# Leaving masked block pairs out of the value products of a hybrid decoder layer, with the last stage in another order

## What is computed

```python
def masked_softmax(s, mask):
    s = jnp.where(mask, s, -jnp.inf)
    ...
    e = jnp.exp(s - m)
    d = jnp.sum(e, axis=-1, keepdims=True)
    return e / jnp.where(d > 0, d, 1.0)
...
# branch "s": selected blocks of 64; SEQ is 1024, so all 16 of them are selected
ms = (top_v > -jnp.inf)[..., None] & (tok <= q_pos[None, :, None, None, None])
...
o_s = jnp.einsum('bqkgns,bqknsd->bqkgd', ps.astype(q.dtype), g[..., 1, :])
# branch "w": sliding window of 512
mw = ((dist >= 0) & (dist <= WINDOW) & (kw_pos[None, :] >= 0))[None, :, None, None, :]
...
o_w = jnp.einsum('bqkgl,blkd->bqkgd', pw.astype(q.dtype), kv_w[:, :, 1])
```

## Time and profile before

| | us |
|---|---|
| median of 3 runs | 885.97 |
| lowest and highest | 880.46, 892.27 |
| span of the profiled execution | 878.0 |
| PE, DVE, ACT, POOL busy in it | 822.5, 520.0, 359.6, 259.9 |

### The profile page before, as it was taken

How to read it: one execution, slowest core, us unless ns; L and a number is a source line. 1 busy time by engine, 2 the same in 40 slices (tenths; PEclk the granted TensorE clock), 3 DMA queues, 4 the chain that set the end, 5 groups by cost and what they waited for, 6 DMA issues and landing times. The chain is left out here.

```text
span 878.0 us, 20078 instructions
## 1 busy us (share of the span) xinstructions
PE 822.5 (94%) x8505; PEld 539.5 (61%) x8505; DVE 520.0 (59%) x1095; ACT 359.6 (41%) x739; POOL 259.9 (30%) x216
## 2 busy tenths in 40 slices
PE   3999999999999999998999998888999989889996
PEld 2457998877788756657555556544646464654553
DVE  2146652376788744457435456686877867757711
ACT  4041002011222245547223337775765656444632
POOL 2048879360000043326311010446211130302021
PEclk8899999999999999999999999899999999999999
DMA  9952265454020000301942452801011010202021
GB/s 302 343 195 104 66 212 206 197 190 165 28 74 1 25 5 1 97 1 49 367 166 62 146 173 63 256 19 29 24 49 51 13 63 6 72 2 74 15 99 49
DMA packets 45411, 89.06 MB, mean 101 GB/s; under 512 B 4388, under 2 KB 26076, under 8 KB 43210
## 3 DMA queue, kind: packets, MB, share of 16 engines
q1 hardware_dynamic: 38202, 54.94, 19.3%
q0 software_dynamic: 6080, 31.79, 10.3%
q10 hardware_dynamic: 1040, 1.05, 0.4%
HBM read 75.49 MB, written 16.40 MB: 105 GB/s over the span
## 5 line engine op out<-in xcount | busy, mean ns | idle before, releaser
L2198 PE MATMUL PS<-W,hT 128*128 128x512 f32 x256 | 113.0, 594 | 0.5 <-DVE W L1819 0.5
L1984 DVE CUSTOM_DVE_ANT_0 PS<-PS,consts 128x640 f32<-128x640 f32 (+5 forms) x96 | 77.3, 837 | 28.7 <-PE PS L2617 28.4
L1103 POOL TENSOR_TENSOR Q<-Q,U 128x512 f32<-128x512 f32 x16 | 20.3, 1268 | 228.4 <-DVE U L2018 228.4
L2198 PEld LDWEIGHTS PS<-W,hT 128*128 128x128 f32 x256 | 47.9, 190 | 56.1 <-issue 54.8
L1431 ACT ACTIVATE hT<-PS,small 128x128 f32<-128x128 f32 (+7 forms) x64 | 47.1, 744 | 47.0 <-DVE small L1984 44.0
L2584 PE MATMUL PS<-U,Y 128*128 128x512 f32 x128 | 60.2, 604 | 0.8 <-ACT Y L1445 0.8
L2584 PE MATMUL PS<-U,Q 128*128 128x512 f32 x128 | 59.3, 601 | 1.3 <-issue 1.3
L1431 ACT ACTIVATE T<-PS,small 128x640 f32<-128x640 f32 (+4 forms) x64 | 41.9, 667 | 30.1 <-DVE small L1984 29.2
L2000 DVE STREAM_TRANSPOSE hT<-hT 128x1024 f32<-128x1024 f32 (+6 forms) x29 | 42.5, 1483 | 2.7 <-ACT hT L1431 2.6
L2584 PEld LDWEIGHTS PS<-U,Q 128*128 128x128 f32 x128 | 23.4, 190 | 32.1 <-issue 32.1
L2617 PE MATMUL PS<-KTsw,W 64*128 64x512 f32 (+3 forms) x128 | 39.4, 519 | 1.6 <-ACT hT L1431 1.3
(11 more groups left out here) (545 smaller groups left out, 1855.3 us busy)
## 6 DMA issues: line engine op xcount, KB each, us to landing
W<-in_w_in SPq DMA_DIRECT2D x4, 2048.0 KB, 7.7
W<-in_w_ada SPq DMA_DIRECT2D x7, 1024.0 KB, 16.1
U<-in_x_prompt SPq DMA_DIRECT2D x8, 512.0 KB, 11.3
W<-in_w_ada SPq DMA_DIRECT2D x2, 2048.0 KB
U<-in_state_win_kv POOLq DMA_DIRECT2D x8, 512.0 KB
W<-in_x_prompt SPq DMA_DIRECT2D x8, 512.0 KB, 3.5
out_y_prompt<-W SPq DMA_DIRECT2D x8, 512.0 KB, 3.4
out_new_win_sample<-in_state_win_kv POOLq DMA_DIRECT2D x1, 4032.0 KB, 24.1
```

Source lines behind the costliest of these rows:

```text
L1103: nc.gpsimd.tensor_tensor(Q3[:, i, :], Q3[:, i, :], spare, ALU.add).then_inc(s_added, 1)
L1984: ins = nc.vector.tensor_tensor_reduce(x, x, strip(u), 1.0, -NEG, ALU.add, ALU.min, sneg_m[u % 2][:, m:m + 1])
L2198: ins = nc.tensor.matmul(bank(z_bank(u)), hT3[:, k, i * P:(i + 1) * P], w, start=(k == 0), stop=(k == KT8 - 1))
```

## The change

A step of a value group leaves out the pairs (j, b) that the mask empties. A new function says which key blocks query block j needs, and the first and last of them carry start and stop:

```diff
+        def key_blocks(u, again, j):
+
+            if again == VALUE_TILES[u] - 1:
+                return 0, j + 1
+            if u % 2 and u // 2 >= WIN // P and again == 0:
+                return j, 4
+            return 0, 4
...
                     for b in range(4):
                         for j in range(4):
+                            lo, hi = key_blocks(u, again, j)
+                            if not lo <= b < hi:
+                                continue
                             q, c = slice(32 * j, 32 * j + 32), again * P + 32 * b
                             for kv in range(KVH):
                                 ins = nc.tensor.matmul(bank(4 + j, 0, P)[HALF[kv]].rearrange("p (g q) -> p g q", g=GQ),
                                                        VREP[k, a + again][q, b * P + kv * HD:b * P + kv * HD + HD],
                                                        PROB[k][q, kv * GQ:kv * GQ + GQ, c:c + 32],
-                                                       start=(again == 0 and b == 0), stop=(last and b == 3))
+                                                       start=(again == 0 and b == lo), stop=(last and b == hi - 1))
```

And ORDER is another string with the same letters, each as often as before:

```diff
-            "qqssxsxyxwmtsvcxtqksysxvxcszsxxwkgstmstxvvcsaxykuwsxtmootooogaxtoootssrrvxppvctxtskusvxtpvxsvcqxopos"
-            "xsostppxpxqpkttsnsyorxoogxottosrvvvttcxsknxavsvvvcstxtuwsxxoqsstmkoxxftosstxoxossgoxtxooyrsrvxvssfvt"
-            "vxcaxstxwmkussxxvvststvvxxvsscxqkxosxtosnsoyxosxtstooxwxssrtgoxxossmrxvvxvsastvvtcxxkussvvxxtnsxvssf"
-            "xvsxxsxvyvsstcoxxqwossmotoxosxgstttoxroxaokssrnxvvxvsstvvctxxkussfxvvtvsxvsxvxvvssctooxtsxgtxsoxorks"
-            "sxvvvxsxvvcatytssoxouoxoftrssoxkoooxsnsrwtxoxossgomxxorbasxvvstsxvvxstxduttvvofvnhvcokvvfovvvcorkogo"
-            "obaodurnhofoooroooornhf")
+            "sqqxsswxysxmvstxtcxyzsqkxtcxtsvsgxmkxcwtsavvysswxuxgkttsopaopoxomrorooxtoscptvvtskusxvvvxpcpspsqxxpo"
+            "potxskxqttxtoyssrtonoosxxstcroxgosvvtvtkxsavscvxvvtsufxxwskxmotnsoxssyoxtgttxoqxstrsorooxosxanstxvvs"
+            "svvxsctsxwfxmukssxxtxvvxscgxstvtxftxyvvsxorxxsotstsoxxmqkossorxoxwsasocxoxstsvvssvvtvkusxsxvntxvsxtx"
+            "sxxcyvxxtxsxvmssvgvssqkoossaofxtwsstxtrooooorxsvtxvnscxsvtvvxskussxxvvxxgssvxxcvfxssvtvvaxtstsotkour"
+            "xxooxcssvyxvmvsnsvvxswrsooxkotooxosxtgsxoossxorooottrbsasxvvsxxsbvvsxtduvvoxvvtnocfvvcvtodthkvvookgf"
+            "aoooounrohroooroofnorhf")
```

## The result

| | before | after |
|---|---|---|
| median of 20 runs each, us | 886.18 (878.41 to 892.27) | 875.81 (871.95 to 881.55) |
| ratio, 95% interval | | 0.9889 [0.9869, 0.9910] |
| span of the profiled execution, us | 878.0 | 879.7 |

The change makes the kernel 9.8 us faster by the ratio, 10.4 by the medians: 1.1%, less than the 2% that the chances were put to, yet its interval is clear of 1. Forecast were -7.8 us and 878.2.

What follows compares the result with a forecast made beforehand. PE was taken to bound the last stage, its dense value steps limited by instruction packets. Terms -8 - 1 + 2 - 0.8 = -7.8 us gave span 870.2 and median 878.2 us (chance 0.48), range 868 to 890.

Steps and rivals of the forecast that it cites:

- the 2% that the chances were put to: Whole kernel: change distinguishable from none, 17.7 us; faster by more 0.10, slower 0.04, within 0.86.
- Term 1: Value products in the last stage: 960 fewer instructions shorten PE's waits for instruction packets, -8 us (0 to -13.9).
- the walk over the packets: Step-by-step count of value-step supply losses, one packet per 3.7 us: 25.8 us lost before, 12.6 after.
- Term 2: Array time of diagonal value steps: the fullest tile still has 8 records, so only -1 us.
- Rival B: Value steps: array time falls in proportion to records, sum -13.6 us, 872 us; chance 0.13.
- Term 3: Waits under the new order: less cover at the score units for the softmax chain, +2 us.
- Term 4: End of the last stage: PE's idle for ACT's copy before the last output product is covered, -0.8 us.
- Reordering alone some 3: Last stage: new order without leaving pairs out saves some 3 us of the instruction-supply loss.
- (A): Last stage: fetch is not the limit, or ACT and DVE waits eat the gain; 886 us, chance 0.22.
- (C): Score units: each of 11 new short distances meets a DVE transpose, +14.3 us; 891.5 us, chance 0.12.
- (D): Value products: pairs are not left out, or the wrong ones, so only reordering acts; 884 us, chance 0.05.
- the 8.0 us that the forecast carried over from span to median: Whole kernel: before's median 885.97 us lay 8.0 above its profiled span 878.0; added to the predicted span 870.2.

Runs made afterwards that it cites:

- tiny: Changed kernel, but each masked pair issued with one query per head (4 columns) instead of left out; 885.80 us, ratio 1.0024 to before.
- skip_only: After's value products with masked pairs left out, but before's issue order; 874.71 us, ratio 0.9868 to before.
- order_only: The kernel before with after's issue order and all 64 records in every value step; 881.13 us, ratio 0.9975.
- balanced: Changed kernel with as many pairs left out, spread so no row group has over three key blocks (wrong results); 875.17 us, ratio 0.9884 to before.
- skip_tail: skip_only with its last letters of the order as in after (Y half transposed early, quarter output product ahead); 872.81 us, ratio 0.9842 to before.
- tiny2: tiny with each small product of the masked pairs issued twice, 960 more PE instructions; 903.98 us, ratio 1.0198 to before.
- pad512: Changed kernel plus 512 redundant PE waits among the sparse 128x512 products before the last stage; 876.66 us, ratio 0.9886 to before.
- after_again: The changed kernel run once more, on the same chip as skip_tail; 877.33 us, ratio 0.9887 to before.
- shift80: Changed kernel plus 80 redundant waits ahead of the last stage, moving the packet borders; 875.99 us, ratio 0.9887 to before.
- shift224: Changed kernel plus 224 redundant waits ahead of the last stage, moving the packet borders; 877.98 us, ratio 0.9912 to before.

## Why the prediction came out right

**Term 1, right in its mechanism, too small in its size.** Forecast: -8 us for 960 instructions, between 0 and -13.9, with nearly all of it in the old order. Measured: -11.7 in the old order. tiny is what shows the mechanism: the same pairs as after, the same count as before, and the gain is gone; and the holes end at a fixed distance behind the packets. That the small products cost array time instead is ruled out by tiny's own steps (2.02 or 2.03 us for two, after 2.02). The forecast took half of the open holes (7 us) plus a little for the breaks hidden inside runs; measured are 11.7 us in the old order (before to skip_only), 11.9 between after and tiny and 7.6 between after and order_only: 2.0 to 3.2 per packet, of the 3.7 that were its upper end. So the step that was off is the choice inside the bounds: half of the open holes is what the trace shows (13.9 to 8.4 us, 5.5), but the runs gained more, up to twice that. Where the rest goes is seen only in part (below).

**What failed inside term 1** is the walk over the packets. It gave the forecast a ratio of 0.45 to 0.49; with its borders moved it forecast +3 to 5 and -2 to 4 us, and neither came. What counts by the runs is how many instructions a dense stretch has, not where a packet ends in it.

**Term 2, right.** Forecast: -1, the fullest tile sets the time. Measured: 0.08 for a step alone, 0.01 inside a run of two, and 0.22 in balanced, where the fullest tile really has less. Rival B (6.8 us, by proportion) falls by the timeline.

**Term 3, right in size as far as it can be read.** Forecast: +2, at the score units, for ACT. In the trace the idle with a releaser went from 14.4 to 14.7 us in the last stage, with the 0.8 of term 4 gone in it: +1.1. Only a part is where it was put. The score products' waits for ACT went from 4.6 to 5.5 us, +0.9: less at the large units (L2625 has 1.3 and 0.4 us, of which L2617 had 2.8 in all), but 3.1 us at the small ones (L2621), where the old order had 1.1:

```profile
PE PS L2613 <- ACT hT L1431: 0.7, 2, 0.6
PE PS L2613 <- ACT KcTs L1423: 0.4, 1, 0.4
```

The rest is at the value products, which wait 2.1 us longer for DVE (3.9 to 6.0), less what is saved elsewhere. By the runs the new order costs 1.9 us beside skip_only and 4.0 beside skip_tail, but at like clock less than 1 beside skip_only, and beside skip_tail on the same chip. "Reordering alone some 3" came out as 2.2 less with an interval that includes zero, and was not additive. A likely reason, not tested: with the pairs gone the holes that a better order could fill were gone as well.

**Term 4, right.** The gap of 0.80 us is gone in after and in skip_tail. The runs give 2.3 us for it, with overlapping intervals; skip_tail's runs had a mean clock of 0.991, skip_only's 0.988, and at like clock 0.7 us is left.

**The rivals.** (A), fetch hidden or eaten by the next wait, 886 us: it falls by tiny, tiny2 and the 875.81 measured. The Trainium skill ("Runtime: NRT & Kernel Launch", Instruction fetch mechanics) says that the fetch is hidden; these runs agree only where instructions are sparse (pad512, 512 for nothing) and contradict it in the value steps. (C), 891.5 us, falls: no wait for the scores' chain grew by over 10 us. (D) falls: 480 products fewer.

**What stays open.** The profiled executions give -5.0 us for the last stage of after, the runs about -10; for skip_only it is -7.7 against -11.7. Much of the difference in spans is the draw, that is, which execution the profiler caught: the profiled execution of after took 881.55 us for a span of 879.7, 1.9 around it, and is its slowest run of 20; with the same 1.9, before's took about 880, 6 under its median. (So the 8.0 us that the forecast carried over from span to median was mostly the draw too.) Another part goes by PE's clock, which is below full for 23.0 us in after's last stage, 22.7 in after_again, 13.5 in skip_only and 11.2 before. In after and in after_again alike, two of these stretches (6.9 us of the 11.8 more than before) stand right behind open holes, and one of 6.9 us behind a wait of 1.26 us for DVE (to 572.53 in after). skip_only has an open hole of 1.97 us too and no low clock behind it; why one hole is followed by a low clock and another is not was not tried. The mean clock of the runs says the same as the traces: after_again 0.978 to 0.990, skip_tail 0.985 to 0.996. So much of what the new order loses beside the old one may go by the clock; no run changes the clock alone, so this is not shown.

## What to carry to other kernels

Where PE issues many small packed products, count its instructions (loads and waits too) per microsecond and hold them against the packets of the instruction queue: holes without a releaser in the middle of a run of equal products are the sign. There, work left out pays by the instruction and not by the array: 960 fewer brought 1.1 to 1.3%, though they freed next to no array time, while 512 more (waits, long met) in a sparse stretch cost nothing. To check that it is supply, see whether the holes end at one distance behind the packets of that queue. And read the granted clock of the runs beside their times before a difference of a few microseconds is put down to a change. To save array time in a packed step, take records from the fullest tile; and try such a cut in the old order first, since a new one brings waits of its own.

## What the runs showed of the hardware that was not expected

- Where the instructions are dense, a product of 4 columns is no cheaper than one of 128 columns: tiny 1.0024, order_only, the same order with full products, 0.9975.
- 256 instructions cost 2.0 us (after to order_only), 3.1 (skip_only to before), 3.2 (after to tiny) and 4.1 us (tiny to tiny2) in the dense stage, where packets came one per 3.7 us, and 0 in the sparse one (pad512, waits).
- PE's open holes end at a fixed distance behind a packet of q8: 1.3 to 1.5 us in 11 of 12 before and 6 of 6 after.
- Open holes can be followed by a stretch at half clock: 3.4 us each behind holes of 2.60 and 1.79 us in after. Two steps inside the second, at 769.39, took 2.98 us where 2.02 is the rule at full clock.
- A packed step of 64 products and one of 40 take the same time if the fullest tile has 8 in both (2.02 and 2.01 us for two steps); with 6 in it the step is 0.22 us shorter.
- Where the packet borders fall made no difference that could be measured (shift80 0.9887, shift224 0.9912, after 0.9889).
